# An exchange of softmax statistics moved to VectorE, and several moved orders, in a hybrid decoder layer

## The chip, the cores and the metric

The kernel runs on one core of a Trainium2 chip. The metric is the device time of one execution in microseconds; the figure that counts is the median over runs.

## What is computed

One decoder layer over 512 tokens with 1024 features, all in float32: a half-step SwiGLU network, a mixer with two parallel branches, a second half-step SwiGLU network, and a final RMS norm.

```python
x = x + 0.5 * swiglu(rms_norm(x, ffn1_norm), ...)          # D_FF = 2816
h = rms_norm(x, mix_norm)
c_q, c_kv, k_rope, q_d, k_d, v_d, g_a, g_b = split(h @ w_in)
y_a = latent_attention(rms_norm(c_q) @ w_uq, rms_norm(c_kv) @ w_ukv, rope(k_rope)) @ w_br_mla   # 8 heads, causal
outs, lses = three dilated groups of 8 heads each (strides 1, 4, 16), T5 bias, banded causal
w = softmax(stack(lses), axis=0)                            # weights of the three groups, per token and head
y_b = sum(w * outs) @ w_br_dil
x = x + (sigmoid(g_a + b_a) * y_a + sigmoid(g_b + b_b) * y_b) @ w_out
x = x + 0.5 * swiglu(rms_norm(x, ffn2_norm), ...)
y = rms_norm(x, norm_final)
```

What matters here is the softmax `w` over three groups: group 0 has its statistics (maximum and sum of each query) in token order, groups 1 and 2 have them by phase of the stride, so that before the weights can be made each kind must be brought into the other's order.

## The kernel before

Activations lie feature-major, 128 features on the partitions and 512 tokens along a row. Every product is made of three float32r matmuls: weights are loaded by SyncE into one of four `raw` buffers (`load`), rounded by ScalarE into `w_hi` (`split_hi`), the remainder taken by VectorE into `w_lo` (`split_lo`), two such pairs being in use at a time; then `multiply` makes hi*hi, hi*lo and lo*hi. A piece is 8 tiles of 128 x 128 weights, so 24 matmuls of 512 columns. The pieces form one stream, laid out in `PIECES`: up1, down1, latent, mla, dil, merge, out, up2, down2. Each engine runs its own program in a written order, and semaphores that count pieces (`piece_done`, `hi_ready`, `lo_ready`), taken outputs (`chunk_taken`) and so on join them; an engine never takes a later step before an earlier one.

- **Start.** SyncE loads eight chunks of `x_t` and the first pieces. ScalarE and VectorE round a chunk of `x` before TensorE uses it; the second piece needs chunks 4 to 7.
- **Latent.** Six pieces of `w_latent`. Between them TensorE makes column sums (`token_sums`) and spreads the reciprocal roots over the partitions (`spread`). VectorE's `take_mean` and `take_root` and ScalarE's `mean_root` make a root from the sums.
- **mla.** Eight heads. A head has scores, softmax (`maxima`, `exponentials`, `normalize`), transposes of the probabilities (`turn_probs`), the product with the values (`attend`), and, to cover the softmax, the next head's latent projection and a gate's projection. The last head has the first dilated projection as its cover, and calls `turn_probs` for parts 0 and 1 after six of its eight tiles.
- **dil.** Four turns (`dilated_pair`), each for two heads of each group: ten projections of a piece each (query, key for three groups, three values, one gate) and a last gate in two halves. Scores come after projections 2, 4 and 6. Behind projection 8, TensorE moves the statistics with eight matmuls against constant 0/1 matrices (`C_FOLD`, `C_EXPAND`) into bank 7, VectorE picks the wanted ones with masks and sums (`group_weights`), and scales the probabilities (`scale_probs`). `take_dil_probs` on ScalarE copies eight units of transposed probabilities out of the banks.
- **merge.** The eight chunks of `mixed` (four of each branch) are rounded to `act_hi`, `act_lo` and multiplied with the branch weights.
- **End.** Column sums of the squares, one root, two spreads over 512 columns; VectorE scales six chunks, GpSimd two, and SyncE stores them.

Of the kernel before, what the change touches and what calls it, by code (L numbers as in the profile page):

```python
# [25 lines left out]
F32 = mybir.dt.float32  # L26
F32R = mybir.dt.float32r
I32 = mybir.dt.int32
ALU = mybir.AluOpType
# [54 lines left out]
WARM_UP = 3  # L84

# [41 lines left out]
C_IDENT, C_ONES, C_EXPAND, C_FOLD = 0, P, 2 * P, 2 * P + SEQ  # L127
C_MOD = C_FOLD + SEQ
C_DIV = C_MOD + BLOCKS
C_CAUSAL = C_DIV + BLOCKS  # L130
# [29 lines left out]
def shape_constants():  # L160
# [3 lines left out]
    j = np.arange(SEQ)  # L164
# [3 lines left out]
    c[:, C_EXPAND:C_EXPAND + SEQ] = p[:, None] == j[None, :] // 4  # L168
    c[:, C_MOD:C_MOD + BLOCKS] = p[:, None] % 4 == np.arange(4)

    c[:, C_FOLD:C_FOLD + SEQ] = p[:, None] == (4 * (j % P) + j // P)[None, :] % P
    c[:, C_DIV:C_DIV + BLOCKS] = p[:, None] // 32 == np.arange(4)
# [10 lines left out]
    onehot = np.zeros((NUM_BUCKETS, T5_END), np.float32)  # L183
    mask = np.full((GROUP_HEADS, T5_END), NEG_INF, np.float32)
    for g, stride in enumerate(STRIDES):
# [5 lines left out]
        onehot[bucket[ok], at[ok]] = 1.0  # L191
        mask[:, at[ok]] = 0.0
    return c, onehot, mask


def decoder_layer(nc, x_t, positions, rel_bias, gains_in, tables, onehot_in, mask_in, ffn, w_latent, w_lora_up,
# [22 lines left out]
    with ctx:  # L219
# [33 lines left out]
        exchanged = work[:, 3, 0:6 * 4 * 2 * BLOCKS]  # L253
# [11 lines left out]
        t5_onehot = shared("t5_onehot", [NUM_BUCKETS, T5_END])  # L265
        t5_mask = shared("t5_mask", [GROUP_HEADS, T5_END])
        t5_row = shared("t5_row", [GROUP_HEADS, T5_END])
        t5_rel = shared("t5_rel", [NUM_BUCKETS, GROUPS * GROUP_HEADS])
# [70 lines left out]
        stats_moved, weight_ready, weight_exp = sem("stats_moved"), sem("weight_ready"), sem("weight_exp")  # L339
# [50 lines left out]
        def _(sp):  # L390
# [103 lines left out]
        def _(pe):  # L494
# [21 lines left out]
            def up_turn(f, turn, i, first=False):  # L516

                for q in range(4):
# [10 lines left out]
                    for k in range(HALF):  # L529
# [5 lines left out]
                        if first and f == 0 and q == 2 and k == 1:  # L535
# [15 lines left out]
                    if first and f == 0 and q == 3:  # L551

                        pe.wait_ge(table_loaded, 48)
                        for g in range(GROUPS):
                            last = nc.tensor.matmul(bank[4 + g][0:GROUP_HEADS, 0:T5_LEN[g]],
                                                    t5_rel[:, g * GROUP_HEADS:(g + 1) * GROUP_HEADS],
                                                    t5_onehot[:, T5_AT[g]:T5_AT[g] + T5_LEN[g]], start=True, stop=True)
                        last.then_inc(setup_pe, 1)
# [1190 lines left out]
```

## Time and profile before

| | |
|---|---|
| median of 3 runs | 1302.68 us (1302.43 to 1305.31) |
| profiled execution | 1302.95 us, of which the span of the trace is 1301.2 us |
| TensorE busy | 1279.7 us, 98% |
| VectorE, ScalarE busy | 662.1 us (51%), 442.4 us (34%) |
| mean DMA rate | 91 GB/s |
| mean granted TensorE clock | 0.995 |

Matmuls overlap in the records: each of 512 columns lasts some 0.39 us, but the next one starts 0.23 us behind it. So the time between starts is what a matmul costs, and the duration of one record is not. In the chain that ended last that cost is what is counted. A float32 matmul (not float32r) shows as two records.

### The profile page before, as it was taken

To read this page: it belongs to the slowest core of one execution; us is meant where nothing else is said; L and a number is where in the kernel's file an instruction comes from. 1 tells how busy PE (TensorE), PEld (TensorE's weight loads), DVE (VectorE), ACT (ScalarE), POOL (GpSimd) and SP (SyncE) were. 2 spreads that over 40 slices of the span, in tenths; PEclk is the share of its full clock that TensorE was granted. 3 is DMA by queue.
4 is the path that set the end of the run, shared out by engine and by line. 5 is a ranking of instruction groups with operands and counts; after the bars stand their busy time and mean duration, and the time that the engine had idled before them with its cause. 6 is when DMAs were issued, how large, how long until landed. Compare 5 with 4: busy or idle time off the path is not lost.

```text
span 1301.2 us, 16722 instructions
## 1 busy us (share of the span) xinstructions
PE 1279.7 (98%) x6054; PEld 1039.0 (80%) x6054; DVE 662.1 (51%) x943; ACT 442.4 (34%) x763; POOL 18.7 (1%) x36
## 2 busy tenths in 40 slices
PE   8999999999999999999999999999999999999997
PEld 6788888888887777787878878788888888888886
DVE  5654444433345677564554646676644444443322
ACT  5322222322232445343333334423433333322221
POOL 0000000000000000300000000000000000000000
PEclk9999999999999999999999999999999999999998
DMA  6342222233322122512222221123322232233331
GB/s 226 98 111 97 97 97 96 89 89 103 91 91 70 63 69 65 129 66 81 80 67 83 78 81 64 65 97 97 101 96 95 96 96 97 97 91 92 100 89 65
DMA packets 36066, 118.87 MB, mean 91 GB/s; under 512 B 4680, under 2 KB 4680, under 8 KB 36032
## 3 DMA queue, kind: packets, MB, share of 16 engines
q1 hardware_dynamic: 34416, 114.83, 27.7%
q0 software_dynamic: 1328, 3.56, 1.5%
q8 instruction: 20, 0.33, 0.1%
q14 instruction: 14, 0.11, 0.0%
q10 hardware_dynamic: 288, 0.03, 0.0%
HBM read 115.85 MB, written 2.55 MB: 91 GB/s over the span
## 4 chain that ended last, share of the span: by engine, by line
PE 94%; DVE 3%; ACT 1%; issue 1%; DMA 1%; SPq 0%; POOL 0%; POOLq 0%; ACTq 0%; DVEq 0%
PE bank L545 37%; PE bank L378 17%; PE bank L380 16%; PE bank L379 16%; PE bank L728 1%; PE bank L751 1%; ACT w_hi L360 1%; PE bank L649 1%; PE bank L676 1%; DVE mla_stats L1437 1%; PE bank L665 1%; PE bank L768 1%; PE bank L764 1%; DVE w_lo L365 0%; PE bank L512 0%
## 5 line engine op out<-in xcount | busy, mean ns | idle before, releaser
L365 DVE TENSOR_TENSOR w_lo<-raw,w_hi 128x1024 fp32r<-128x1024 f32 (+2 forms) x221 | 259.1, 1172 | 241.9 <-ACT w_hi L360 240.0
L360 ACT ACTIVATE w_hi<-raw 128x1024 fp32r<-128x1024 f32 (+2 forms) x221 | 224.3, 1015 | 441.5 <-PE bank L545 230.4
L545 PE MATMUL bank<-act_hi,w_hi 128*128 128x512 f32 x704 | 218.5, 392 | 3.5 <-DVE act_lo L1161 3.5
L545 PE MATMUL bank<-act_lo,w_hi 128*128 128x512 f32 x704 | 217.4, 390 | 0.0
L545 PE MATMUL bank<-act_hi,w_lo 128*128 128x512 f32 x704 | 217.1, 390 | 0.0
L378 PE MATMUL bank<-act_hi,w_hi 128*128 128x512 f32 x528 | 211.9, 401 | 2.9 <-DVE mla_vt L1430 1.5
L380 PE MATMUL bank<-act_hi,w_lo 128*128 128x512 f32 x528 | 206.2, 390 | 0.0
L379 PE MATMUL bank<-act_lo,w_hi 128*128 128x512 f32 x528 | 205.9, 390 | 0.0
L545 PEld LDWEIGHTS bank<-act_hi,w_hi 128*128 128x128 f32 x704 | 132.1, 188 | 32.6 <-DVE w_lo L365 3.9
L545 PEld LDWEIGHTS bank<-act_lo,w_hi 128*128 128x128 f32 x704 | 132.6, 188 | 27.9
L545 PEld LDWEIGHTS bank<-act_hi,w_lo 128*128 128x128 f32 x704 | 132.4, 188 | 27.7
L378 PE MATMUL bank<-hid_hi,w_hi 128*128 128x512 f32 x352 | 136.9, 389 | 0.0
L379 PE MATMUL bank<-hid_lo,w_hi 128*128 128x512 f32 x352 | 136.9, 389 | 0.0
L380 PE MATMUL bank<-hid_hi,w_lo 128*128 128x512 f32 x352 | 136.9, 389 | 0.0
L378 PEld LDWEIGHTS bank<-act_hi,w_hi 128*128 128x128 f32 x528 | 99.1, 188 | 28.7 <-issue 4.8
L380 PEld LDWEIGHTS bank<-act_hi,w_lo 128*128 128x128 f32 x528 | 99.1, 188 | 21.5
L379 PEld LDWEIGHTS bank<-act_lo,w_hi 128*128 128x128 f32 x528 | 99.3, 188 | 18.6
L1246 DVE TENSOR_TENSOR work<-bank,rstd 128x512 f32<-128x512 f32 x44 | 30.4, 692 | 123.4 <-PE bank L545 123.2
L379 PEld LDWEIGHTS bank<-hid_lo,w_hi 128*128 128x128 f32 x352 | 66.1, 188 | 13.8
L380 PEld LDWEIGHTS bank<-hid_hi,w_lo 128*128 128x128 f32 x352 | 66.1, 188 | 13.7
L378 PEld LDWEIGHTS bank<-hid_hi,w_hi 128*128 128x128 f32 x352 | 66.1, 188 | 13.6
L921 ACT ACTIVATE hid_hi<-work 128x512 f32 (+1 forms) x44 | 27.8, 632 | 94.8 <-DVE work L1252 94.8
(173 smaller groups left out, 1058.9 us busy)
## 6 DMA issues: line engine op xcount, KB each, us to landing
raw<-in_ffn_up SPq DMA_DIRECT2D x87, 512.0 KB, 3.4
raw<-in_w_dil SPq DMA_DIRECT2D x40, 512.0 KB, 3.4
raw<-in_ffn_down SPq DMA_DIRECT2D x32, 448.0 KB, 3.3
raw<-in_ffn_down SPq DMA_DIRECT2D x16, 512.0 KB, 3.5
raw<-in_w_mla_gates SPq DMA_DIRECT2D x8, 512.0 KB, 3.4
raw<-in_w_branches SPq DMA_DIRECT2D x8, 512.0 KB, 3.4
raw<-in_w_out SPq DMA_DIRECT2D x8, 512.0 KB, 3.4
raw<-in_w_latent SPq DMA_DIRECT2D x6, 512.0 KB, 3.4
```

Source lines behind the costliest of these rows:

```text
L360: nc.scalar.activation(w_hi[:, s % SPLIT, 0:tiles * P], raw[:, s % RAW, 0:tiles * P], ACT.Copy).then_inc(hi_ready, 1)
L365: nc.vector.tensor_tensor(w_lo[:, s % SPLIT, 0:tiles * P], raw[:, s % RAW, 0:tiles * P], w_hi[:, s % SPLIT, 0:tiles * P].bitcast(F32), ALU ...
L378: nc.tensor.matmul(out, a, hi(k), start=first, stop=False)
L379: nc.tensor.matmul(out, a, lo(k), start=False, stop=False)
L380: last = nc.tensor.matmul(out, b, hi(k), start=False, stop=end)
L545: last = nc.tensor.matmul(out, w[:, s % SPLIT, tile * P:(tile + 1) * P], moving[:, row, :], start=row == 0 and w is w_hi and moving is act_hi,
L649: nc.tensor.matmul(out, mla_q[0:QK_DIM, h % 2, b * P:(b + 1) * P], mla_k[0:QK_DIM, h % 2, 0:(b + 1) * P], start=True, stop=False, skip_gro ...
L665: last = nc.tensor.transpose(bank[5 + unit % 2][:, at:at + P], mla_p[:, row * P:(row + 1) * P], ident)
L676: last = nc.tensor.matmul(bank[7][V_DIM * e:V_DIM * (e + 1), key * P:SEQ], mla_v[:, e, key, :], probs_t[:, e, at:at + width], start=key == ...
L728: last = nc.tensor.matmul(out, dil_q[rows, g, b * P:(b + 1) * P], dil_k[rows, g, keys], start=True, stop=True, skip_group_check=True)
L921: nc.scalar.activation(hid_hi[:, bass.ds(2 * i + 2 * turn + j, 1), :], work[:, 3:4, :], ACT.Copy).then_inc(hid_rounded, 1)
L1246: nc.vector.tensor_tensor(work[:, 0, :], bank[c % UP_BANKS][:, :], rstd[:, :], ALU.mult).then_inc(chunk_taken, 1)
```

## The change

1. **The exchange goes to VectorE.** The eight statistics matmuls of a turn, their constants and VectorE's masks and sums are taken out. `fold_stats` (behind the maxima of group 1) brings group 0's statistics into phase order with two 32 x 32 block transposes and eight copies; `expand_stats` (ahead of the split for projection 9) brings those of groups 1 and 2 into token order with two transposes and twelve copies. `group_weights` and `scale_probs(0)` come one piece earlier, ahead of the take of projection 8, and ScalarE's exponential of the weights with them.
2. **Start.** The second piece is loaded ahead of chunks 4 to 7 of x. The constants table is 384 columns wide where it was 1416. The first column sums and the first spread come one step later each.
3. **Position rows.** The three products of `t5_rel` and `t5_onehot` contract over 32 rows each; they lie on partitions 0 to 31, 32 to 63 and 64 to 95 now, where all lay on 0 to 31.
4. **Latent.** The mean and root of the keys come ahead of the next split; their spread two tiles later. Behind the last latent piece, the addition of the rotated key and the query root come behind `take_key_value`.
5. **Last latent head.** Its cover is two dilated projections, and the transposes of parts 0 and 1 stand in the second.
6. **Last turn.** The last dilated turn is written out of the loop, and in it ScalarE and VectorE round the four latent chunks of `mixed`. In every turn ScalarE's split for the next piece stands behind the copy of unit 5, where it stood behind unit 4.
7. **End.** Four matmuls of 512 columns (`keep_warm`), whose result nothing reads, stand behind each of the two column sums.

```diff
@@ sync
             load_x(3)
+            sp.wait_ge(x_loaded[0], 16)
+            load(sp, 1, 0, ffn[0][0][1], TILES)
             for k in range(HALF, KM):
-                sp.wait_ge(x_loaded[k - HALF], 16)
+                sp.wait_ge(x_loaded[k - HALF + 1], 16)
                 load_x(k)
-                if k == HALF + 1:
-                    sp.wait_ge(x_loaded[2], 16)
-                    load(sp, 1, 0, ffn[0][0][1], TILES)
@@ tensor
-                        if first and f == 0 and q == 2 and k == 1:
+                        if first and f == 0 and q == 2 and k == 2:
...
-                        if first and f == 0 and q == 2 and k == 3:
+                        if first and f == 0 and q == 3 and k == 0:
...
-                            last = nc.tensor.matmul(bank[4 + g][0:GROUP_HEADS, 0:T5_LEN[g]],
-                                                    t5_rel[:, g * GROUP_HEADS:(g + 1) * GROUP_HEADS],
-                                                    t5_onehot[:, T5_AT[g]:T5_AT[g] + T5_LEN[g]], start=True, stop=True)
+                            rows = slice(g * NUM_BUCKETS, (g + 1) * NUM_BUCKETS)
+                            nc.tensor.matmul(bank[4 + g][0:GROUP_HEADS, 0:T5_LEN[g]], t5_rel[rows, :],
+                                             t5_onehot[rows, 0:T5_LEN[g]], start=True, stop=True).then_inc(setup_pe, 1)
...
-                    if q == 4 and k == 2:
+                    if q == 4 and k == 4:
                         spread(2, rstd_keys, bank[4])
...
-                    project(PIECES["dil"], 0, c, bank[c % 2][:, :], turn_early)
+                    project(PIECES["dil"], 0, c, bank[c % 2][:, :])
+                    project(PIECES["dil"] + 1, 0, c + 1, bank[(c + 1) % 2][:, :], turn_early)
...
-                pe.wait_ge(dil_exp, 24 * i + 24)
-                for b in range(BLOCKS):
-                    nc.tensor.matmul(bank[7][:, b * 16:(b + 1) * 16], const[:, C_FOLD + b * P:C_FOLD + (b + 1) * P],
-                                     stats[:, :, 0, 0, :], start=True, stop=True, skip_group_check=True)
-                for b in range(BLOCKS):
-                    last = nc.tensor.matmul(bank[7][:, 64 + b * 32:96 + b * 32], ...
-                last.then_inc(stats_moved, 1)
...
+            def keep_warm():
+                for _ in range(KEEP_WARM):
+                    nc.tensor.matmul(bank[4][:, :], w_hi[:, 0, 0:P], hid_hi[:, 0, :], start=True, stop=True)
+
             token_sums(sumsq, bank[7], stop=False)
+            keep_warm()
             pe.wait_ge(squared, 4 * KM + KQ + KKV)
             token_sums(square, bank[7], start=False).then_inc(norm_full, 1)
+            keep_warm()
@@ vector
+            def fold_stats(i):
+                dve.wait_ge(dil_exp, 24 * i + 8)
+                nc.vector.transpose(squares, stats[:, :, 0, :, :].rearrange("p t o n -> p t (o n)")).then_inc(own, one())
+                dve.wait_ge(own, so_far())
+                for u in range(BLOCKS):
+                    last = nc.vector.tensor_copy(by_stat[:, :, 8 * u:8 * u + 8], squares[SQ * u:SQ * (u + 1), :]...)
...
+                nc.vector.transpose(by_token, work[0:SQ, 3, 4 * SQ:8 * SQ]).then_inc(own, one())
+                dve.wait_ge(own, so_far())
+                for b in range(BLOCKS): ...
+            def expand_stats(i):
+                dve.wait_ge(dil_exp, 24 * i + 24)
+                for b in range(BLOCKS):
+                    for t in range(2): ...                      # 8 copies
+                nc.vector.transpose(work[0:SQ, 3, 4 * SQ:8 * SQ], by_token).then_inc(own, one())
+                for u in range(BLOCKS): ...                     # 4 copies
+                nc.vector.transpose(stats[:, :, 1:3, 0, :], squares).then_inc(own, one())
...
                 for q in range(12):
+                    if q == 8:
+                        expand_stats(i)
                     split_lo(dve, s + q + 1, d, tiles)
                     if q in (3, 5, 7):
                         dil_maxima(q // 2 - 1, i)
+                    if q == 5:
+                        fold_stats(i)
+                    if q == 8:
+                        group_weights(i)
+                        scale_probs(0)
...
                     if q == 9:
-                        group_weights(i)
-                        scale_probs(0)
+                    if final and q == 10:
+                        split_mixed(0)
+                        split_mixed(1)
```

**SyncE, the start of the program.** `x<-in_x_t` is a chunk of x, `raw<-in_ffn_up` a piece of weights. Before:

```order
L414 DMA x<-in_x_t 128x512 x2
L414 DMA x<-in_x_t 128x512 [waits x_loaded0]
L414 DMA x<-in_x_t 128x512 [waits x_loaded1]
L353 DMA raw<-in_ffn_up 128x1024 [waits x_loaded2]
L414 DMA x<-in_x_t 128x512 [waits x_loaded2]
L414 DMA x<-in_x_t 128x512 [waits x_loaded3]
L353 DMA raw<-in_ffn_up 128x1024 [waits x_loaded5]
L353 DMA raw<-in_ffn_up 128x1024
```

After the change:

```order
L410 DMA x<-in_x_t 128x512 x2
L349 DMA raw<-in_ffn_up 128x1024 [waits x_loaded0]
L410 DMA x<-in_x_t 128x512 [waits x_loaded1]
L410 DMA x<-in_x_t 128x512 [waits x_loaded2]
L410 DMA x<-in_x_t 128x512 [waits x_loaded3]
L410 DMA x<-in_x_t 128x512 [waits x_loaded4]
L349 DMA raw<-in_ffn_up 128x1024 [waits x_loaded5]
L349 DMA raw<-in_ffn_up 128x1024
```

The load of the second piece (the first `128x1024` one) has moved ahead of chunks 4 to 7, and each of these waits for one chunk more.

**VectorE, a dilated turn, from the take of projection 7 to that of projection 8.** `w_lo` is the split for the next projection, `dil_vt` the take of a value projection, `dil_p` the scaling of the probabilities. Before:

```order
L1541 TENSOR_TENSOR dil_vt<-bank,rstd 128x128x4 [waits piece_done]
L365 TENSOR_TENSOR w_lo<-raw,w_hi 128x1024 [waits hi_ready]
L1541 TENSOR_TENSOR dil_vt<-bank,rstd 128x128x4 [waits piece_done]
L365 TENSOR_TENSOR w_lo<-raw,w_hi 128x512 [waits hi_ready]
L1552 TENSOR_TENSOR work<-bank,const 128x64 [waits stats_moved]
L1552 TENSOR_TENSOR work<-bank,const 128x128
L1560 TENSOR_REDUCE stats<-work 128x4 [waits own]
L1563 TENSOR_REDUCE stats<-work 128x4 x2
```

After the change:

```order
L1467 TENSOR_TENSOR dil_vt<-bank,rstd 128x128x4 [waits piece_done]
L1579 COPY work<-stats 32x2x4x2 [waits own,dil_exp]
L1579 COPY work<-stats 32x2x4x2 x7
L1583 STREAM_TRANSPOSE work<-work 32x128 [waits own]
L1586 COPY work<-work 32x4x8 [waits own]
L1586 COPY work<-work 32x4x8 x3
L1590 STREAM_TRANSPOSE stats<-work 128x2x2x8 [waits own]
L361 TENSOR_TENSOR w_lo<-raw,w_hi 128x1024 [waits hi_ready]
L1597 TENSOR_TENSOR neg_top<-stats 128x16 [waits own]
```

Between the take of projection 7 and the split for projection 9 there are fourteen small instructions now, of which the first waits for the exponentials; the weights follow ahead of the take of projection 8 (not shown: the same seven instructions and four of `scale_probs`).

**VectorE, the last latent head.** `mla_p` is the scaling of the probabilities by `normalize`; the `w_lo` behind it is the split for the second dilated projection. Before:

```order
L1450 TENSOR_SCALAR mla_p<-mla_p,mla_stats 128x384
L1450 TENSOR_SCALAR mla_p<-mla_p,mla_stats 128x512
L365 TENSOR_TENSOR w_lo<-raw,w_hi 128x1024 [waits hi_ready]
L1455 COPY mixed<-bank 128x512 [waits pv_done]
L1541 TENSOR_TENSOR dil_q<-bank,rstd 128x512 [waits piece_done]
L365 TENSOR_TENSOR w_lo<-raw,w_hi 128x1024 [waits hi_ready]
L1541 TENSOR_TENSOR dil_k<-bank,rstd 128x512 [waits piece_done]
```

After the change:

```order
L1458 TENSOR_SCALAR mla_p<-mla_p,mla_stats 128x384
L1458 TENSOR_SCALAR mla_p<-mla_p,mla_stats 128x512
L361 TENSOR_TENSOR w_lo<-raw,w_hi 128x1024 [waits hi_ready] x2
L1467 TENSOR_TENSOR dil_q<-bank,rstd 128x512 [waits piece_done]
L1472 COPY mixed<-bank 128x512 [waits pv_done]
L1664 MEMSET stats 128x2x8
L1467 TENSOR_TENSOR dil_k<-bank,rstd 128x512 [waits piece_done]
```

The split for the second projection stands where it stood, behind `normalize`; a second split (for the third projection) and the take of the first projection are ahead of the copy of `mixed`.

## Rows read from the trace of the kernel before

**Rows 1.** The page: busy time, share of the span, instructions.

```profile
PE 1279.7 (98%) x6054; PEld 1039.0 (80%) x6054; DVE 662.1 (51%) x943; ACT 442.4 (34%) x763; POOL 18.7 (1%) x36
```

**Rows 2.** Waits of TensorE over the run: us in total, times, longest.

```profile
PE bank L545 <- DVE act_lo L1161: 3.5, 1, 3.5
PE bank L512 <- DVE token_rstd L1353: 1.9, 1, 1.9
PE bank L378 <- DVE mla_vt L1430: 1.5, 2, 1.2
...
PE bank L768 <- ACT probs_t L1081: 1.3, 4, 0.4
PE bank L665 <- DVE mla_p L1450: 1.3, 1, 1.3
...
PE bank L378 <- DVE act_lo L1631: 0.5, 1, 0.5
PE bank L378 <- DVE work L1640: 0.4, 1, 0.4
```

**Rows 3.** Timeline of SyncE's queue, 0 to 20 us: start, us, instruction.

```profile
2.61 2.78 SPq L414 DMA_DIRECT2D x<-in_x_t  x4
7.11 0.33 SPq L353 DMA_DIRECT2D raw<-in_ffn_up  x1
```

**Rows 4.** Timeline of ScalarE, 12 to 14 us; idle before, releaser in brackets.

```profile
12.24 1.06 ACT L360 ACTIVATE w_hi<-raw 128x1024 fp32r<-128x1024 f32 x1 [3.70 <-DMA raw<-in_ffn_up]
```

**Rows 5.** Windows at the start: busy us by engine, granted clock (PEclk), DMA.

```profile
12.00:15.30 3.30, 0.00 (x0) 0.00 (x0) 1.97 (x3) 3.06 (x4) 0.27 (x1) 1.00 1.00 381
15.30:18.80 3.50, 3.44 (x9) 2.70 (x10) 3.12 (x4) 3.50 (x6) 2.58 (x5) 0.53 0.93 314
```

**Rows 6.** Chain that ended last, whole run: start, us, what.

```profile
27.72 0.89 PE bank L512 x8
...
35.45 1.60 PE bank L555 x6
37.05 217.85 PE bank L545 x960
...
563.50 1.09 PE bank L728 x16
...
596.55 0.87 PE bank L751 x8
...
664.82 0.80 PE bank L823 x8
665.62 0.91 PE bank L826 x8
...
1290.81 2.67 PE bank L512 x16
```

**Rows 7.** Timeline of VectorE, 655 to 676 us, the second dilated turn.

```profile
658.49 1.10 DVE L1541 TENSOR_TENSOR dil_vt<-bank,rstd 128x512 f32<-128x512 f32 x1 [1.81 <-PE bank L380]
660.50 1.23 DVE L365 TENSOR_TENSOR w_lo<-raw,w_hi 128x1024 fp32r<-128x1024 f32 x1 [0.91 <-ACT w_hi L360]
...
667.06 0.17 DVE L1560 TENSOR_REDUCE stats<-work 128x4 f32<-128x16 f32 x1
...
668.10 0.17 DVE L1568 TENSOR_TENSOR neg_top<-stats 128x16 f32<-128x16 f32 x1
...
670.06 2.23 DVE L1594 TENSOR_TENSOR dil_p<-dil_p,weight 128x128 f32<-128x128 f32 x4
```

**Rows 8.** Timeline of VectorE, 415 to 418.7 us, behind the last latent piece.

```profile
416.12 0.68 DVE L1401 TENSOR_TENSOR mla_k<-mla_k,rotated 32x512 f32<-32x512 f32 x1
...
417.24 0.68 DVE L1429 TENSOR_TENSOR mla_k<-bank,rstd_kv 64x512 f32<-64x512 f32 x1
```

**Rows 9.** Timeline of VectorE, 530 to 536 us, the last latent head.

```profile
533.23 1.27 DVE L1450 TENSOR_SCALAR mla_p<-mla_p,mla_stats 128x128 f32<-128x128 f32 x4
534.41 1.22 DVE L365 TENSOR_TENSOR w_lo<-raw,w_hi 128x1024 fp32r<-128x1024 f32 x1
```

More of the change, by code:

```diff
@@ L84 @@
 WARM_UP = 3
+KEEP_WARM = 4
 POOL_CHUNKS = 2
@@ L1101, in dilated_pair @@
                     take_dil_probs(unit, i)
+                    if final and unit == 3:
+                        act.wait_ge(piece_done, PIECES["merge"] - 1)
+                        round_mixed(0)
+                        round_mixed(1)
+                    if final and unit == 5:
+                        round_mixed(2)
                     if unit == 1:
                         gate_tanh(c + e + 9, MLA_HEADS + 2 * i)
-                    if unit == 4:
+                    if unit == 5:
                         split_hi(act, s + 12, d, TILES)
             dilated_pair(0, first=True)
-            with act.Fori(1, PAIRS) as i:
+            with act.Fori(1, PAIRS - 1) as i:
                 dilated_pair(i)
+            dilated_pair(PAIRS - 1, final=True)
+            round_mixed(3)
             act.wait_ge(piece_done, PIECES["merge"])
-            for k in range(2 * PAIRS):
-                if k == PAIRS:
+            for k in range(PAIRS, 2 * PAIRS):
+                if k == 2 * PAIRS - 1:
                     gate_tanh(CHUNKS["merge"] - 1, 2 * KM - 1)
-                act.wait_ge(mixed_taken, k + 1)
-                nc.scalar.copy(act_hi[:, k, :], mixed[:, k, :]).then_inc(mixed_rounded, 1)
+                round_mixed(k)
             with act.Fori(0, KM // 4) as i:
@@ new lines, in expand_stats @@
+            def expand_stats(i):
+                dve.wait_ge(dil_exp, 24 * i + 24)
+                dve.wait_ge(own, so_far())
+                for b in range(BLOCKS):
+                    for t in range(2):
+                        target = by_token.rearrange("q (v t g b e) -> q b t g v e", v=BLOCKS, b=BLOCKS, t=2, g=2)
+                        last = nc.vector.tensor_copy(
+                            target[:, b, t], stats[SQ * b:SQ * (b + 1), t, 1:3, 1, :].rearrange("q g (v e) -> q g v e", e=2))
+                last.then_inc(own, one())
+                dve.wait_ge(own, so_far())
+                nc.vector.transpose(work[0:SQ, 3, 4 * SQ:8 * SQ], by_token).then_inc(own, one())
+                dve.wait_ge(own, so_far())
+                for u in range(BLOCKS):
+                    last = nc.vector.tensor_copy(squares[SQ * u:SQ * (u + 1), :].rearrange("i (q v) -> i v q", v=BLOCKS),
+                                                 by_stat[:, :, 8 * u:8 * u + 8])
+                last.then_inc(own, one())
+                dve.wait_ge(own, so_far())
+                nc.vector.transpose(stats[:, :, 1:3, 0, :], squares).then_inc(own, one())
@@ L1600, in dilated_pair @@
                     tiles = HALF if q in (9, 10) else TILES
-                    if q or not first:
+                    if q == 8:
+                        expand_stats(i)
+                    if q > 1 or not first:
                         split_lo(dve, s + q + 1, d, tiles)
```

156 lines of the change are left out of this document (75 added, 81 removed).

## The prediction

> **What bounds the kernel now.** I read the page first: TensorE is busy 98% of the span [rows 1], so only two things shorten it: fewer or cheaper matmuls, and shorter waits of TensorE. VectorE and ScalarE, at half and a third, count only where TensorE waits for them. The table of TensorE's waits comes next [rows 2]: all of them together are some 12 us, the largest 3.5 us, once, at the start. Then the windows [rows 5], where a clock below full shows time lost that no wait shows, and the chain [rows 6] for what a group of matmuls costs from start to start. 960 matmuls in 217.85 us are 0.227 us each [rows 6]; a projection of 24 is 5.45 us. Last, VectorE's timeline around each place that the change touches [rows 7 to 9].
>
> **The change, part by part.** The sum is made against the profiled execution, 1302.95 us; the median is 0.27 us lower, so I take the sum off 1302.68.
>
> *Exchange.* The matmuls go: 0.80 + 0.91 = 1.71 us of the chain in each of four turns [rows 6], 6.84 us. It is a gain only if VectorE's work stays hidden. The fourteen new instructions of `expand_stats` cannot start before the take of projection 7 ends, 658.49 + 1.10 = 659.6 [rows 7]. Behind them comes the split for projection 9 (1.23 us [rows 7]), and TensorE wants it when the transposes of the values are through, at 664.82, where the statistics matmuls stand now [rows 6]. So the exchange may last 664.8 - 1.25 - 659.6 = 3.9 us before TensorE waits. Its price: no transpose or 32-partition copy of this size is in the trace. The nearest are small ones: thirteen instructions start between 667.06 and 668.10, 0.09 us each [rows 7], so fourteen take 1.2 us; with every one waiting for the last (0.17 to 0.25 us) 3 us. From above, a 32-row instruction of 512 elements takes 0.68 us [rows 8], which gives 9.5 us for fourteen. The new ones have 16 to 128 elements, nearest to the small ones; most follow each other, four wait: I take 2.0 us, hidden, ending at 661.6. The split ends at 662.9, the weights (668.10 to 670.06, 1.96 us) at 664.9, `scale_probs(0)` (2.23 us) at 667.1, the take of projection 8 (1.1 us) at 668.2 [rows 7]. TensorE needs that take behind projection 9, at 664.8 + 5.45 = 670.3: 2 us to spare. The small instructions taken out behind it (1.0 us, 667.06 to 668.10) and the earlier scaling give back time. `fold_stats` has ten such instructions, 1.4 us, and sits in an idle like the 1.81 us before the take [rows 7]; its result is used a whole projection later. Its cover gone, the take of a key comes up to 1 us late, still long before the scores. Cost 0.
>
> *ScalarE's copy.* TensorE waits 1.3 us in four turns for copies of probabilities [rows 2]; in the code this is unit 5 behind a 1.06 us split, which now comes after it. The next piece is not wanted before two more units. Gain 1.3 us (bounds 0 and 1.6).
>
> *Start.* TensorE is through with the first piece 3.5 us before it can begin the second [rows 2], at about 15.3 us [rows 5]. ScalarE had waited for that piece's landing until 12.24 [rows 4]; it was issued at 7.11 [rows 3], so it took 5.1 us, and another 3.1 us passed until TensorE ran. Now it is issued third in the row of four loads that starts at 2.61 and lasts 2.78 us [rows 3], by 4.0 us. With the same 5.1 + 3.1 us TensorE runs at 12.2 where it is free at 11.8: 3.1 us gained. Then the clock: after the idle 3.3 us, the next 3.5 us ran at a granted 0.53 [rows 5], that is at the 1.2 GHz level, which cost 3.5 x 0.47 = 1.65 us. With 0.4 us idle I expect no fall: 4.75 us in all. Against it stand the things that were hidden under those 5 us: the last chunks of x, whose loads wait for one chunk more, the third piece, the constants, the column sums. I let them take back 0.75 us and count 4.0 us. Bounds: 0.5 us if chunks and sums come as late as now, 5.2 us if nothing is late.
>
> *Position rows.* The three products take 1.60 us [rows 6]. On two row groups, the scores show what sharing gives: eight matmuls of 128 columns (sixteen records) on alternating 64-row halves take 1.09 us, four on all 128 rows (eight records) 0.87 us [rows 6], so 0.136 against 0.217 us each. With that ratio 1.60 becomes 1.0: gain 0.6 us. The Trainium skill, TensorEngine Tiling (Array Packing), section Overview, promises up to 4x for contractions of 32 rows or fewer, since such tiles run side by side. By that rule the three would take as long as the longest, an estimate of 0.7 us, and the sum would be 0.3 us lower. The pairs' ratio of 1.6 where the page allows 2 speaks for the lesser gain. Bounds 0 and 1.0 us.
>
> *Latent.* The spread of the keys' root waits 1.9 us [rows 2], since VectorE makes mean and root behind a split and its operands are ready earlier. They go ahead of it, and the spread six matmuls (1.4 us) later: all 1.9 us gone. Behind the last latent piece the gate's projection waits for `take_key_value` (longest 1.2 us [rows 2]); from 416.12 to 417.24 VectorE does the key's addition and root [rows 8], which now come later: 1.1 us less. The query is then made 1.1 us later relative to the key, under a projection of 5.45 us. Gain 3.0 us.
>
> *Last latent head.* The wait of 1.3 us before the transposes [rows 2] ends with `normalize`, at 534.5 [rows 9]. The transposes now wait for nothing, but the second projection needs its split, which VectorE makes behind `normalize`: 534.41 + 1.22 = 535.63 [rows 9]. TensorE would get there at 534.5 - 1.3 + two tiles (1.36) = 534.6, so it waits 1.1 us. The wait moves; it doesn't go. Gain 0.2 us (bounds 0 and 1.3).
>
> *Merge.* Two waits, 0.5 and 0.4 us [rows 2], with short steps between them: TensorE wants a chunk every three matmuls, 0.68 us, and the first comes late. With four chunks ready beforehand both go. I add 0.4 us for what start-to-start times lose beside the record: 1.3 us (bounds 0.9 and 1.5).
>
> *End.* Both spreads take 2.67 us for sixteen records, eight took 0.89 early in the run [rows 6]: 0.9 us is lost, a lower clock by the end. Four warm matmuls are 0.91 us each time, in idle times of about 0.7 us, so they delay by 0.2 to 0.4 us. The second spread feeds only GpSimd's two chunks, and VectorE's last chunk is nearly as late. Gain 0.4 us (bounds -0.5 and 0.8).
>
> Sum: 6.84 + 1.3 + 4.0 + 0.6 + 3.0 + 0.2 + 1.3 + 0.4 = 17.6 us. 1302.68 - 17.6 = **1285.1 us**.
>
> **The rivals.**
> - *The start gives little.* For it: loads at the start share one bandwidth (381 GB/s and a DMA share of 1.00 between 12 and 15.3 us [rows 5]), so an earlier weight piece makes x later, and TensorE could stop at chunks 5 to 7 or at the sums, with a slow clock again. Against it: until 11.8 us it needs less data than is moved. With 0.5 us in place of 4.0: 1288.6 us. Chance 0.15.
> - *VectorE is late in the turns.* If the exchange costs more than 3.9 us, TensorE waits for the split. At 6 us it is 2.1 us a turn: 1285.1 + 8.4 = 1293.5 us. For it: fourteen instructions, none of which the trace prices, and cross-partition copies. Against it: 16 to 128 elements. Chance 0.09.
> - *Slower than before*, the same mechanism at its upper price: the other gains are 17.6 us or 4.4 us a turn, so it decides from 3.9 + 4.4 = 8.3 us on, each instruction at 0.6 us. At 9.5 us the wait is 5.6 us a turn: 1285.1 + 22.4 = 1307.5 us. Chance 0.02.
> - *The moved orders don't do what they should*: the key's root, the merge and the unit 5 keep their waits because another operand was last. Without 1.3, 1.3 and 1.9 us: 1289.6 us. Chance 0.07.
> - The forecast: 0.67.
>
> **How the numbers follow.** The likeliest case by itself spans 1282 to 1288: all upper bounds (start 1.2, position rows 0.4, head 1.1, end 0.4) would give 1282, the lesser ones of start, end and copy 1288. The range of 8 in 10 reaches on to the first and last rival, 1281.5 to 1290.5; 1293.5 and 1307.5 are left out. A change under 0.2% (2.6 us) can't be told from none here. Faster needs less than 1300.1, which all cases but the slower one give, and a part of the second: faster 0.96, same 0.02, slower 0.02.
>
> **What will show it.** In the profile after: no statistics matmuls, and TensorE's waits without an entry for the split `w_lo` in the turns; VectorE's exchange under 3.9 us from first copy to last transpose. Each turn 2.0 us shorter. TensorE starts on the second piece near 12.2 us, granted clock 1.00 from there. The wait of 1.9 us gone. A wait for `w_lo` of about 1.1 us in the last latent head in place of the one for `mla_p`. No wait at the merge, and spreads of 0.9 us at the end. Wrong would be made of: a start that is short of chunks of x, or an exchange of 4 us and more.

## The result and the profile after

| | before | after |
|---|---|---|
| median | 1302.74 us (1302.43 to 1305.31, 4 runs) | 1285.28 us (1284.85 to 1287.54, 4 runs) |
| span of the trace | 1301.2 us | 1283.7 us |
| mean granted clock of TensorE | 0.995 | 0.999 |

The ratio is 0.9865, with a 95% interval of 0.9848 to 0.9882: 17.5 us less. The profile's page of the kernel after (busy time, share, instructions), beside [rows 1]: TensorE has 56 matmul records fewer and waits 1% of the time, VectorE has 41 instructions more and 7.5 us more work.

```profile
PE 1270.7 (99%) x5998; PEld 1031.0 (80%) x5998; DVE 669.6 (52%) x984; ACT 442.9 (35%) x763; POOL 18.8 (1%) x36
```

The waits of TensorE after, beside [rows 2] (us in total, times, longest):

```profile
PE bank L582 <- DVE work L1308: 1.5, 1, 1.5
PE bank L374 <- DVE w_lo L361: 1.2, 1, 1.2
PE bank L540 <- DVE act_lo L1170: 0.8, 2, 0.4
PE bank L540 <- DVE w_lo L361: 0.8, 2, 0.5
PE bank L374 <- DVE mla_vt L1438: 0.4, 1, 0.4
PE bank L499 <- DVE sumsq L1329: 0.3, 1, 0.3
```

Gone are the 3.5 us at the start, the 1.9 us for the keys' root, the 1.3 us for copies of probabilities, the two at the merge and two of 0.7 us at the end. The 1.3 us for `mla_p` has become 1.2 us for `w_lo`. Small waits at the start are new; they differ between executions (in experiment 11, the same kernel, only the one behind the position rows is left, 0.3 us).

**Where the 17.5 us came from.** The chain that ended last has the same landmarks in both traces, so the gain up to each can be read off. These are the landmarks after, and behind them three of those before:

```profile
33.57 217.94 PE bank L540 x960
...
376.63 0.79 PE bank L499 x8
...
407.59 0.79 PE bank L499 x8
...
417.70 0.70 DVE work L1306
...
519.45 0.48 PE bank L643 x2
...
543.78 1.72 PE bank L723 x16
...
819.53 1.02 PE bank L746 x8
...
910.66 5.45 PE bank L540 x24
```

```profile
550.66 1.72 PE bank L728 x16
...
835.04 1.02 PE bank L751 x8
...
927.68 5.45 PE bank L545 x24
```

| up to | before | after | gain so far | this part | forecast |
|---|---|---|---|---|---|
| loop of up1 entered (start, position rows) | 37.05 | 33.57 | 3.48 | 3.48 | 4.6 |
| first sums of latent | 380.01 | 376.63 | 3.38 | -0.10 | 0 |
| third sums of latent (keys' root) | 413.18 | 407.59 | 5.59 | 2.21 | 1.9 |
| take of the first gate (behind the last latent piece) | 424.50 | 417.70 | 6.80 | 1.21 | 1.1 |
| last head begins | 526.24 | 519.45 | 6.79 | 0 | 0 |
| first dilated scores (last head) | 550.66 | 543.78 | 6.88 | 0.09 | 0.2 |
| last transposes of the last turn (exchange, copy) | 835.04 | 819.53 | 15.51 | 8.63 | 8.14 |
| up2 begins (merge) | 927.68 | 910.66 | 17.02 | 1.51 | 1.3 |
| end of the span | 1301.2 | 1283.7 | 17.5 | 0.48 | 0.4 |

The chain of before does not pass through the start of the third sums. TensorE's timeline has it at 413.02, and at 407.43 after, 0.16 us ahead of the chain; with the same 0.16 us the table has 413.18.

**The exchange on VectorE.** VectorE's timeline in the second turn, beside [rows 7]:

```profile
649.51 1.09 DVE L1467 TENSOR_TENSOR dil_vt<-bank,rstd 128x512 f32<-128x512 f32 x1 [1.82 <-PE bank L376]
650.45 0.97 DVE L1579 COPY work<-stats 32x16 f32<-32x16 f32 x8
651.45 0.30 DVE L1583 STREAM_TRANSPOSE work<-work 32x128 f32<-32x128 f32 x1
651.78 0.79 DVE L1586 COPY work<-work 32x32 f32<-32x32 f32 x4
652.60 0.21 DVE L1590 STREAM_TRANSPOSE stats<-work 128x32 f32<-128x32 f32 x1
652.74 1.19 DVE L361 TENSOR_TENSOR w_lo<-raw,w_hi 128x1024 fp32r<-128x1024 f32 x1
...
655.79 2.23 DVE L1622 TENSOR_TENSOR dil_p<-dil_p,weight 128x128 f32<-128x128 f32 x4
657.94 1.09 DVE L1467 TENSOR_TENSOR dil_vt<-bank,rstd 128x512 f32<-128x512 f32 x1
```

From 650.45 to 652.81 the fourteen instructions take 2.36 us. TensorE wants the split when its transposes (655.41, 0.44 us) are through, at 655.85; it is ready at 653.93. So 1.9 us were to spare, and the exchange could have lasted 2.36 + 1.9 = 4.3 us by this row.

**The start.** SyncE's queue, beside [rows 3], then TensorE's timeline (idle before and releaser in brackets):

```profile
3.57 0.43 SPq L349 DMA_DIRECT2D raw<-in_ffn_up  x1
```

```profile
12.70 0.70 PE L540 MATMUL bank<-act_hi,w_hi 128*128 128x512 f32 x2 [0.36 <-DVE act_lo L1170]
...
18.85 0.73 PE L540 MATMUL bank<-act_hi,w_hi 128*128 128x512 f32 x2 [0.46 <-DVE w_lo L361]
...
22.20 1.02 PE L499 MATMUL bank<-const,sumsq 128*128 128x1 f32 x8 [0.34 <-DVE sumsq L1329]
...
32.48 0.81 PE L551 MATMUL bank<-t_onehot,t_rel 32*8 32x383 f32 x6
33.57 0.74 PE L540 MATMUL bank<-act_hi,w_hi 128*128 128x512 f32 x2 [0.29 <-DVE w_lo L361]
```

The second piece starts 2.66 us earlier (12.70 against 15.36, from the chain before), and the clock is full from there, where [rows 5] has 0.53 between 15.3 and 18.8 us:

```profile
15.36 8.68 PE bank L545 x30
```

```profile
15.00:18.80 3.80, 3.39 (x15) 2.46 (x14) 2.79 (x4) 2.77 (x4) 2.05 (x4) 1.00 0.88 314
```

Its load was issued at 3.57; TensorE's next steps wait for the third piece, the sums' operand and the fifth piece.

One pair of traces does not fix this gain. The changed start was traced six times with the narrow table and three row groups (the changed kernel and experiments 3, 4, 6, 9 and 11), and the loop of up1 was entered between 32.27 and 33.57 us; the pair above has the latest of them. The old start has 37.05 us here and 36.00 us in experiment 1. So start and position rows together gave 2.4 to 4.8 us, depending on which two executions are compared.

### The profile page after: what moved, and what is told of

Same layout as the page of the kernel before. It is cut to its first block, busy times and chain, and to the rows that moved or that the text cites. A ratio compares the mean times of both kernels' runs of the same rounds, so it can differ in the third digit from the quotient of the medians.

```text
span 1283.7 us, 16607 instructions
## 1 busy us (share of the span) xinstructions
PE 1270.7 (99%) x5998; PEld 1031.0 (80%) x5998; DVE 669.6 (52%) x984; ACT 442.9 (35%) x763; POOL 18.8 (1%) x36
## 4 chain that ended last, share of the span: by engine, by line
PE 94%; DVE 2%; DMA 1%; issue 1%; ACT 1%; SPq 0%; DVEq 0%; ACTq 0%
PE bank L540 36%; PE bank L374 17%; PE bank L376 17%; PE bank L375 17%; PE bank L723 1%; PE bank L746 1%; PE bank L643 1%; PE bank L670 1%; DMA x<-in_x_t 1%; DVE mla_stats L1445 1%; PE bank L763 1%; PE bank L659 1%; PE bank L759 1%; ACT w_hi L356 0%; PE bank L732 0%
```

## The experiments

Ratios are against the kernel before, on the same chip. Diffs of the first two are against the kernel before, those of the others against the changed one where nothing else is said.

**1. The exchange alone** (`fold_stats`, `expand_stats`, the earlier `group_weights` and `scale_probs(0)`; orders, loads and tables as before).

```diff
+                    if q == 8:
+                        expand_stats(i)
                     split_lo(dve, s + q + 1, d, tiles)
+                    if q == 5:
+                        fold_stats(i)
+                    if q == 8:
+                        group_weights(i)
+                        scale_probs(0)
```

> The kernel before with the exchange alone moved to VectorE (matmuls out, the two transposing routines in, weights and first scaling one piece earlier, the exponential of the weights with them); the table of constants stays wide. Theory (the exchange is hidden, the matmuls were on the path): four turns shorter by 1.7 to 1.85 us each, so 6.8 to 7.4 us in all, about 1295.6 us, and no wait of TensorE for a split in the turns. Rival (part of the 2.2 us that a turn lost came from the copy of unit 5 and the matmuls overlapped with something): under 5 us, above 1297.7 us. Rival (VectorE is late without the other moves): TensorE waits for w_lo and the time stays above 1299 us.

Measured: 1294.91 us, ratio 0.9941 (0.9923 to 0.9959). A turn went from 76.15 to 74.36 us (first scores to first scores of the second and third turns): 1.79 us less where 1.71 was counted. TensorE waits for no `w_lo` in the turns, and the wait for the copies (1.3 us in four turns) is still there. Four turns make 7.2 of the 8.2 us between the medians.

In the changed kernel a turn takes 73.95 us; the other 0.41 us belong to the order of the copies. This run's wait at the start was 2.4 us, not 3.5, since its second piece landed at 11.23 and not at 12.24; the start differs by about 1 us between executions of unchanged code.

**2. The order of the loads alone.** As in the diff of `@@ sync` above, with the wide table.

> The kernel before with the order of the first loads alone changed; the table of constants stays 1416 columns wide and the first column sums stay behind the second of their piece's rows. Theory (the narrow table and the later sums are what lets the earlier start be kept): the second piece starts near 12.7 us at full clock, then TensorE waits some 3 us at the first column sums for the constants (issued near 16.5 us, landing 7 us later), and 1 to 1.5 us are left: 1301.4 us. Rival (the constants are in time; the sums wait for VectorE's last addition, ready near 22.1 us): a wait of 1.3 us and 3 us gained: 1299.7 us. Rival (the order of loads gives all by itself): 4.3 us gained, 1298.4 us.

Measured: 1305.93 us (10 runs), ratio 1.0018 (1.0008 to 1.0027): slower than before by about 3 us (2.7 between the spans of the two traces). TensorE's timeline, and windows (behind the five busy times the granted clock, the DMA share and GB/s):

```profile
23.32 1.05 PE L503 MATMUL bank<-const,sumsq 128*128 128x1 f32 x8 [3.88 <-DMA const<-in_tables]
```

```profile
23.00:25.00 2.00, 1.68 (x11) 1.56 (x12) 0.18 (x1) 0.53 (x2) 0.00 (x0) 0.94 0.36 124
25.00:29.00 4.00, 4.00 (x14) 3.16 (x13) 1.23 (x1) 1.97 (x2) 0.00 (x0) 0.60 0.18 30
```

The second piece starts at 12.30 (12.70 in the changed kernel), but the first sums then want `const` (the ones they multiply with), issued at 15.69 and landed at 23.28, 7.6 us later. The wait takes back what the earlier piece gave, and the clock falls behind it: 4.0 x 0.40 + 2.0 x 0.06 = 1.7 us more. The loop is entered at 38.16, 1.1 us later than before.

Another 1.5 us of the 2.7 were lost where this edit changes nothing. TensorE waits 1.92 us for the keys' root in both traces, but only here the clock falls behind that wait (0.50 between 404 and 406 us), and the eight spread matmuls take 2.02 us in the chain where they take 1.16 before:

```profile
403.56 2.02 PE bank L511 x8
```

So the start alone explains 1.1 us of the loss in this trace. It shows that the order by itself gains nothing; since the experiment leaves out the later sums as well as the narrow table, it doesn't say which of the two is needed. Experiment 5 asks for the table alone.

**3. The split ahead of the softmax, in the last latent head.**

```diff
@@ scalar, last head only
+                split_hi(act, s + 2, d, following[0])
                 exponentials(h, i)
-                split_hi(act, s + 2, d, following[0])
@@ vector
-                    normalize(h, i)
                     split_lo(dve, s + 2, d, following[0])
+                    normalize(h, i)
```

> The changed kernel, with both halves of the split for the second dilated projection ahead of the last head's softmax (ScalarE: ahead of the exponentials; VectorE: ahead of normalize). Theory (the wait in this head moved from the transposes to the split): the 1.2 us wait for w_lo goes and nothing takes its place, as the transposes now come six tiles into the second projection: 1284.1 us. Rival (the softmax, 1.1 us later, is waited for at the transposes): no gain, 1285.3 us, and the wait of 1.3 us for mla_p is back.

Measured: 1283.42 us, ratio 0.9848 (0.9831 to 0.9864). From the head's scores to the first dilated scores 22.90 us (518.41 to 541.31), where the changed kernel has 24.33: 1.43 us less. No wait took the place of the one for `w_lo`. (Between the medians it is 1.9 us; the two were measured on different chips, and the start of this trace was 0.9 us earlier.)

**4. The exchange three times.** Its result is the same; only VectorE's time for it is tripled.

```diff
                     if q == 8:
-                        expand_stats(i)
+                        for _ in range(3):
+                            expand_stats(i)
```

> The changed kernel with the second routine of the exchange done three times in a row (the same result each time), 7.0 us on VectorE where one takes 2.35. Theory (it may last 4.1 us in the changed kernel before the split for projection 9 is late): TensorE waits 2.9 us a turn for w_lo, 11.7 us in all: 1297.0 us. Rival (the split is not what is waited for; VectorE has more room): under 1290 us. Rival (VectorE is on the path already, each added microsecond counts): 18.7 us more, 1304 us.

Measured: 1305.59 us (10 runs), ratio 1.0019 (1.0009 to 1.0029), 20.3 us above the changed kernel. The waits, one of them in TensorE's timeline, the window behind it, and the window behind the last of the four:

```profile
PE bank L374 <- DVE w_lo L361: 13.8, 5, 3.3
```

```profile
663.01 0.79 PE L374 MATMUL bank<-act_hi,w_hi 128*128 128x512 f32 x1 [3.04 <-DVE w_lo L361]
```

```profile
662.90:666.30 3.40, 3.29 (x8) 2.66 (x9) 2.88 (x12) 1.25 (x3) 0.00 (x0) 0.54 0.48 154
820.00:826.70 6.70, 6.19 (x15) 4.95 (x16) 5.52 (x14) 1.25 (x3) 0.00 (x0) 0.52 0.23 79
```

Less the 1.2 us of the last head, the waits are 12.6 us, 3.15 a turn, where 2.9 was expected. Behind the wait shown, 3.4 us run at 0.54 (the next window is at 1.00), 1.6 us lost; behind those of the first and third turn it is 1.5 and 1.4 us. Behind the wait of the last turn (3.33 us, hardly longer than the others) the clock stays low twice as long: TensorE works 6.1 us at 0.51 there, and 3.0 us are lost. Together the clock took 7.5 us and the waits 12.6, which is 20.1 of the 20.3 us.

The time is nearest to the last rival's 1304 us, but the mechanism is the theory's: the waits are what it counted, and what brought the time up is the clock behind them, which it left out. Experiment 9 speaks against the rival too: 2.4 us more on VectorE cost 0.8 us there.

**5. The constants at the wide table's place and width**, all else as changed.

```diff
-C_IDENT, C_ONES, C_CAUSAL = 0, P, 2 * P
+C_IDENT, C_ONES, C_CAUSAL = 0, P, 2 * P + 2 * SEQ + 2 * BLOCKS
```

> The changed kernel with the table of constants 1416 columns wide again (the added columns are loaded and used by nothing). Theory (the narrow table is what keeps the early start): the first column sums wait for the constants, issued near 16.6 us and landing 7.6 us later at 24.2, where TensorE gets to them at 21.9: 2.3 us of wait, and if the clock falls after it as in e2, 1.7 us more: 1287.5 to 1289.3 us. Rival (the width costs nothing, since the sums wait for VectorE's addition anyway): 1285.3 us.

Measured: 1289.01 us (1285.67, 1289.88, 1288.13, 1290.06), ratio 0.9892 (0.9875 to 0.9908), 3.7 us above the changed kernel. The profiled execution is the 1285.67, and has only a short wait:

```profile
PE bank L499 <- DMA const<-in_tables: 0.7, 1, 0.7
```

The median says that the narrow table is worth 3.7 us here, but the spread is wide: one execution lost nothing, and the three others (1288.1 to 1290.1 us) lie above all of the changed kernel's. Their mean granted clock was 0.995 to 0.997, where the profiled one had 0.999, so a slow stretch is part of the loss. That it stood behind a wait for `const` as in experiment 2 is argued, not shown, since none of them has a trace.

**6. Without the warm matmuls** (both `keep_warm()` calls taken out).

> The changed kernel without the two groups of four warm matmuls at the end. Theory (they keep the clock up through the spreads and cost nearly nothing): the spreads take 2.67 us for sixteen records again where they take 1.8, the end is 0.5 to 0.6 us later: 1285.8 us, granted clock 0.5 in the second spread. Rival (they only delay): 0.3 us less, 1285.0 us, with a full clock in the spreads. Too small for the medians; the profile from the first column sums of the end on decides.

Measured: 1285.79 us, ratio 0.9865 (0.9849 to 0.9882), 0.5 us above the changed kernel. From the loop of up2 to the end of the span it is 368.12 us (915.88 to 1284.0) against 366.73 (916.97 to 1283.7). The chain of this one, then of the changed kernel:

```profile
1272.70 3.57 PE bank L507 x16
```

```profile
1274.26 0.90 PE bank L507 x8
```

Both spreads now run at half the clock: sixteen records in 3.57 us are 0.223 each, eight in 0.90 are 0.112. In this pair the warm matmuls are worth 1.4 us; the medians show 0.5, within their spread.

The record has three more traces without them, and they disagree. From the loop of up2 to the end, the kernel before takes 367.21 us (933.99 to 1301.2) and experiment 2 takes 367.3; in both the clock fell about 1 us into the spreads. Experiment 1 takes 366.62 us (925.88 to 1292.5): its clock stayed full through both spreads, behind the same two waits of 0.7 us, and it ends as fast as the changed kernel.

```profile
1282.71 1.17 PE bank L517 x8
```

The ten traces with the warm matmuls all lie between 366.7 and 366.8 us. So what they do is to take out a fall of the clock that comes in some executions, worth 0 to 1.4 us, about 0.5 us on average over the four traces without them.

**7. Position rows on one row group again**, executed once.

```diff
-                            nc.tensor.matmul(bank[4 + g][0:GROUP_HEADS, 0:T5_LEN[g]], t5_rel[rows, :],
-                                             t5_onehot[rows, 0:T5_LEN[g]], ...)
+                            nc.tensor.matmul(bank[4 + g][0:GROUP_HEADS, 0:T5_LEN[g]],
+                                             t5_rel[:, g * GROUP_HEADS:(g + 1) * GROUP_HEADS],
+                                             t5_onehot[:, T5_AT[g]:T5_AT[g] + T5_LEN[g]], ...)
```

> The changed kernel with the three position products on partitions 0 to 31 again. Theory (the three run side by side on three row groups; the wait for w_lo of 0.29 us behind them is what their gain uncovered): they take 1.60 us where they take 0.81, the wait for w_lo goes, and the loop is entered 0.5 us later. Rival (row groups share nothing; the shorter record is an artefact): 0.81 stays, or the loop is entered 0.8 us later with the wait still there.

Measured: one time, 1285.91 us. TensorE's timeline:

```profile
32.32 1.67 PE L550 MATMUL bank<-t_onehot,t_rel 32*8 32x383 f32 x6
33.92 0.73 PE L540 MATMUL bank<-act_hi,w_hi 128*128 128x512 f32 x2
```

1.60 us from start to start and no wait, against 0.81 + 0.29 = 1.1 us with three row groups: 0.5 us net.

**8. The constants' load earlier**, on top of experiment 3: GpSimd issues it when the second piece has landed, and the other tables when the third has.

```diff
-            pool.wait_ge(raw_loaded[2], 16)
+            pool.wait_ge(raw_loaded[1], 16)
             pool.dma_start(const[:, 0:C_FREQ], tables[:, 0:C_FREQ]).then_inc(const_loaded, 16)
+            pool.wait_ge(raw_loaded[2], 16)
```

> The kernel of e3 with the load of the constants issued behind the landing of the second piece of weights, where it was behind the third. Theory (in e3 the first column sums wait 0.7 us for the constants, and VectorE's addition is ready shortly after that): the wait for the constants goes, 0.2 to 0.7 us less, 1283.0 us. Rival (0.2 MB more in the same stretch make the third piece of weights later, and TensorE waits for its split instead): 1283.4 us or up to 0.5 us more.

Measured: 1284.67 us, ratio 0.9855 (0.9838 to 0.9871), 1.25 us above experiment 3. The wait for `const` is gone, and another, for the third piece, is longer:

```profile
PE bank L541 <- DVE w_lo L361: 1.6, 2, 1.3
```

ScalarE could start on that piece only at 17.16, where it did at 15.00 in experiment 3. That its load now shares the bandwidth with the constants is the likely reason; in other traces of this start the time varies between 15.0 and 16.5 by itself.

**9. The exchange twice**, the loop of experiment 4 with `range(2)`.

> The changed kernel with the second routine of the exchange done twice in a row, 4.7 us on VectorE where the room before the split is late is 4.1. Theory (in e4 12.3 us of the 20 were waits, 3.1 us a turn, and the rest was TensorE at half clock for some 3.4 us after each wait; a short wait leaves the clock alone): a wait of 0.6 to 0.8 us for w_lo a turn, granted clock 1.00 behind it, 2.4 to 3.2 us in all: 1288.1 us. Rival (any wait in the turns costs clock): the same waits and 1.7 us a turn more, 1295 us. Rival (the room is larger than 4.1 us): 1285.3 us.

Measured: 1288.39 us, ratio 0.9885 (0.9869 to 0.9902).

```profile
PE bank L374 <- DVE w_lo L361: 3.7, 5, 1.2
```

Without the last head's 1.2 us that is 0.63 us a turn. The mean granted clock stays at 0.998, and the medians differ by 3.1 us, 0.78 a turn.

**10. The fifth piece rounded ahead**, on top of experiment 3: in the first turn of up1 the split of the fifth piece stands behind the first of the two hidden chunks, on both engines.

```diff
-                    else:
+                    elif not (first and f == 0):
                         split_hi(act, s + 2, 4 * i, TILES)
...
+                    if first and f == 0 and j == 0:
+                        split_hi(act, s + 4, 0, TILES)      # VectorE: split_lo likewise
```

> The kernel of e3 with both halves of the split for the fifth piece of the first network one step earlier (ScalarE: behind the first silu, ahead of the rounding of the hidden chunk; VectorE likewise). Theory (the 0.3 us wait for w_lo behind the position products is a split that stands behind work that nobody wants yet): that wait goes, 0.3 us less than e3: 1283.1 us, which only the profile can tell. Rival (the hidden chunk's rounding, 1 us later, makes a later split late): no gain or up to 0.5 us lost, with a new wait in the second turn of the loop.

Measured: 1283.02 us, ratio 0.9845 (0.9828 to 0.9861). All of TensorE's waits that are left in this execution, and the timeline behind the position rows, where the wait has gone:

```profile
PE bank L582 <- DVE work L1315: 1.5, 1, 1.5
PE bank L374 <- DVE mla_vt L1445: 0.4, 1, 0.4
PE bank L499 <- DVE sumsq L1336: 0.3, 1, 0.3
```

```profile
31.72 0.81 PE L551 MATMUL bank<-t_onehot,t_rel 32*8 32x383 f32 x6
32.45 0.73 PE L540 MATMUL bank<-act_hi,w_hi 128*128 128x512 f32 x2
```

**11 and 12. The changed kernel and the tenth once more**, on one chip.

> The changed kernel, unaltered, on one chip with e12. Theory: 1285.3 us, 1.5 to 2.5 us above e12. Rival (the gain of e3 and e10 was the chip and the landing of the first loads): within 0.7 us of e12.

> The kernel of e10, unaltered, on one chip with e11. Theory: 1283.1 us. Rival: within 0.7 us of e11.

Measured: 1284.75 us (1284.10 to 1284.97), ratio 0.9859 (0.9844 to 0.9875), and 1283.25 us (1282.64 to 1284.94), ratio 0.9849 (0.9836 to 0.9863). The best version is 1.5 us below the changed kernel in the medians; one of its five runs (1284.94) lies among those of the other. In experiment 12 there are waits at the start again (0.5 us for `const`, 0.4 for `act_lo`), and none behind the position rows or in the last head.

## Why the prediction was right, and where its terms were off

The total came out as forecast, 17.5 us for 17.6. The mechanism was right in each part: every wait that was to go went, and the one that was to move moved. That the total agrees to 0.1 us is luck. In the table the start, the sums and the last head fall short by 1.3 us together, and the other parts exceed the forecast by 1.2. The start alone also varies by about 1 us between executions.

One reading of the forecast was wrong: the waits of [rows 2] add up to 13.3 us with the lines not shown, where it says some 12. No term rests on that sum.

- **Exchange: right.** Fourteen instructions took 2.36 us for 2.0; the room was 3.9 us by the forecast. Experiment 9 doubles them to 4.7 us and TensorE waits 0.63 us, so the true room is 4.1 us, a little less than the 4.3 read off the row above (experiment 4 gives 7.1 - 3.15 = 3.9). Nothing became late behind them: the take of projection 8 ends at 659.03, and TensorE needs it only behind projection 9, at 655.85 + 5.45 = 661.3. `fold_stats` took 2.05 us where 1.4 was counted, before a take that nobody waits for. All four turns together gave 8.63 us for 8.14: the turn of experiment 1 puts 0.08 a turn of it on the exchange, and the rest falls to the order of the copies.
- **Start: too large in this pair of traces.** Start and position rows gave 3.48 us, not 4.6 (2.4 to 4.8 over all traces, so the forecast is within what executions differ by). The load was issued 0.4 us sooner than assumed but took 6.0 us and not 5.1 (ScalarE starts on the piece at 9.57, 9.57 - 3.57); several loads were in flight beside it, which is the likely reason. So the second piece starts at 12.70 and not at 12.2. The clock's 1.65 us came back whole. Of what was to take back 0.75 us, `w_lo` and the sums alone cost 0.6 and 0.5 us from start to start (18.85 and 22.20, each less the start before it and 0.455), and the fifth piece 0.29. 2.66 + 1.65 + 0.79 - 0.6 - 0.5 - 0.29 = 3.7; the 0.2 us to 3.48 is spread over steps under 0.1 us. The step that the forecast did not have is what the late constants cost when the table is wide: it named "the constants" among the things that were hidden and gave them no price of their own. Experiment 2 shows 3.9 us of wait and 1.7 us of clock for them, and experiment 5 a loss of 3.7 us between medians.
- **Position rows: mis-sized, and partly uncovered.** The pairs' ratio gave 1.0 us; the rows take 0.81. The Trainium skill, TensorEngine Tiling (Array Packing), section Overview, whose gain was weighed against that ratio, was nearer: its estimate was 0.7 us, and the trace bears it out but for 0.1. Yet of the 0.79 us gained, 0.29 became a wait for the fifth piece, which the longer products had covered (experiment 7: 0.5 net; experiment 10 takes that wait away).
- **Latent: right.** 2.21 for 1.9 and 1.21 for 1.1; the start of matmuls behind a wait costs some 0.15 us beside the recorded idle time (18.85 and 22.20 above; in experiment 9, 0.78 us a turn for a wait of 0.63), as the forecast allowed for at the merge alone (1.51 for 1.3). Taking out the 1.9 us wait has a second worth that no term had: in experiment 2 the clock fell behind it and 1.5 us more went, in the traces before and of experiment 1 it did not.
- **Last head: right.** The wait moved to `w_lo` and measures 1.2 us for 1.1; the gain was 0.09 us for 0.2. The chain there, beside [rows 9]:

```profile
526.43 1.27 DVE mla_p L1458 x4
527.71 1.15 DVE w_lo L361
...
528.99 0.47 PE bank L374
```

  Experiment 3 shows the cause by taking it away: with the split ahead of the softmax 1.43 us come free.
- **End: right in sum** (0.48 for 0.4), against the trace of before, in which the clock fell in the middle of the spreads. Against experiment 1 the same end gains nothing, and against experiment 6 it gains 1.4 us.
- **VectorE late: the price was too low.** The rival was priced by the wait alone, so that it would decide from 8.3 us on. Experiment 4, at 3 x 2.36 = 7.1 us, is already slower than before (ratio 1.0019): three waits of some 3 us cost 1.4 to 1.6 us of half clock behind them, the fourth 3.0. What was wrong is that 8.3 us and 1307.5 us were worked out from the wait alone. Experiment 9 shows that a wait of 0.6 us has no such price. The rival's other case, 6 us and a wait of 2.1 us a turn, was not tried.

One more reading on VectorE. Four copies of 32x32 took 0.79 us, 0.20 each, and eight of 32x16 took 0.97, 0.12 each, where the small unlinked instructions of [rows 7] started 0.09 us apart. The copies move between partition groups. The Trainium skill, VectorE: DVE Perf Modes, section "Two Vector instructions with no wait between them", says that an instruction is held until all earlier ones of VectorE have finished when its input or output starts in another group of 32 partitions than that of the one before it. Every one of the four changes its group and of the eight every second, and the trace agrees with that in the order of the prices. The sizes differ there, but `fold_stats` has four copies of the smaller size, each of which changes its group:

```profile
636.76 0.70 DVE L1568 COPY stats<-work 32x16 f32<-32x16 f32 x4
```

They take 0.175 us each where the eight of the same size take 0.12, so the size is not what makes the difference. Their access patterns are not the same, and no run changes the group alone.

## What to carry to other kernels

Price a wait of TensorE of 3 us or more with the slow stretch behind it (1.4 to 1.7 us here, once 3.0), and one of 0.6 us amid dense work with itself and the 0.15 us of restart. In between the clock is a matter of the execution: behind 1.9 us it fell in one trace of three, and behind the two waits of 0.7 us around the short column sums at the end in three of four. Where the question is half a microsecond at the start or the end, compare several traces of each kernel, since one pair can mislead by 1 us. An earlier load pays only as far as the data of the next consumers are early too, so follow each load that it passes, and the small table at the end of the queue above all. When a stretch is made shorter, look which load or split it had covered, and, when a wait is moved, ask whether the work that is now last could stand ahead of the step that makes it late.

## What the runs showed of the hardware that was not expected

- The granted clock fell to the 1.2 GHz level behind all waits of 2.4 to 3.9 us (the 2.4 us at the start of experiment 1; 0.54 and 0.60 in the windows of experiments 4 and 2). It fell behind a wait of 1.92 us in experiment 2 and stayed full behind the same wait before and in experiment 1. It fell behind two waits of 0.7 us at the end of three traces (before, experiments 2 and 6) and not in experiment 1. Behind the waits of 0.3 to 1.3 us between full pieces it stayed at 1.00.
- The slow stretch was some 3 to 4 us long in most cases, and 6.7 us in the last turn of experiment 4.
- Three float32 products of 32 rows and 383, 255 and 255 columns on three row groups took 0.81 us, on one 1.60 us: a factor of 2, where the longest alone would allow 2.3.
- A table of constants landed 7.6 us after its issue beside other loads (experiment 2), and the same code's start varied by about 1 us between executions (experiment 1).
